# V of the eight short sequences from one stationary tile of high and low x; the memory weights cast by ScalarE; rotation buffers apart

## The reference, cut to what matters

```
proj = x @ w_in                       # 1024 -> 8192 columns
cb, cc, ch, rq, rk, rv, rg, mq, gl = split(proj)
a_out = (cb * conv3(cc * ch)) @ w_conv_out
q, k = rotary(rq), rotary(rk) * 128**-0.5;  v = rv        # 4 heads, v is 4 x 256 wide
o, new_state = retention(q, k, v, state)                  # chunks of 128, or the 8 positions
b_out = (silu(rg) * groupnorm(o)) @ w_ret_out
mk, mv = split(mem_prompt @ w_mem_kv)                     # prompt only: 256 rows x (512 + 512)
m_out = memory_attention(mq, mk, mv) @ w_mem_out
x = LN(alpha*x + (gates * (a_out, b_out, m_out)).sum() @ w_out)
x = LN(alpha*x + relu(x @ w_up)**2 @ w_down)
```

## Time and profile before

| | us |
|---|---|
| median of three runs | 2241.53 (2239.97 to 2242.13) |
| profiled execution | 2223.44 |
| its span, first to last instruction | 2221.6 |
| PE busy | 2161.7 (97%) |
| POOL busy | 1398.9 (63%) |
| DVE busy | 962.5 (43%) |
| ACT busy | 332.3 (15%) |

### The profile page before, as it was taken

The page is one execution under the profiler, slowest core; times in us unless marked ns, Lnnn a source line. Parts: engine busy times, 40 slices in busy tenths (PEclk is TensorE's granted clock), DMA queues, the critical chain, the costliest instruction groups (busy, mean ns, idle before and its releaser), DMA issues.

```text
span 2221.6 us, 39895 instructions
## 1 busy us (share of the span) xinstructions
PE 2161.7 (97%) x16468; PEld 2116.2 (95%) x16468; DVE 962.5 (43%) x1450; ACT 332.3 (15%) x584; POOL 1398.9 (63%) x1620
## 2 busy tenths in 40 slices
PE   6999999999999999999999999999999999999997
PEld 6998999999998999999999989999999989999996
DVE  6236500443368622324691562005424793324147
ACT  2122101032013100000141220010410221000002
POOL 5743558655684967767666446776456757767672
PEclk9999999999999999999999999999999999999998
DMA  4323524234321223222223153242352212222221
GB/s 159 112 76 97 169 77 134 84 105 133 115 95 58 96 76 96 76 91 80 72 63 104 58 171 114 95 125 73 106 172 78 94 58 95 77 95 76 95 76 43
DMA packets 199794, 214.96 MB, mean 97 GB/s; under 512 B 5233, under 2 KB 192625, under 8 KB 199537
## 3 DMA queue, kind: packets, MB, share of 16 engines
q1 hardware_dynamic: 168832, 170.14, 24.3%
q10 hardware_dynamic: 30832, 42.90, 5.8%
HBM read 199.06 MB, written 13.97 MB: 96 GB/s over the span
## 4 chain that ended last, share of the span: by engine, by line
PE 90%; DVE 6%; POOL 2%; issue 1%; ACT 0%; DMA 0%; POOLq 0%; ACTq 0%; SPq 0%; DVEq 0%
PE gp L405 64%; PE gp L421 7%; PE gp L431 7%; PE qb L500 6%; PE gp L556 5%; POOL w_lo L371 1%; PE qb L531 1%; DVE r L1663 1%; DVE r L1757 1%; DVE r L1666 1%; DVE x_lo L1672 1%; POOL w_hi L368 1%; PE gp L741 1%; DVE dacc L1619 0%; DVE qb L1660 0%
## 5 line engine op out<-in xcount | busy, mean ns | idle before, releaser
L371 POOL TENSOR_TENSOR w_lo<-stage,w_hi 128x256 fp32r<-128x256 f32 x1280 | 1043.0, 845 | 28.0
L368 POOL TENSOR_SCALAR w_hi<-stage 128x1024 fp32r<-128x1024 f32 (+1 forms) x336 | 358.4, 1067 | 755.1 <-PE gp L405 447.0
L405 PE MATMUL gp<-x_hi,w_hi 128*128 128x288 f32 x2176 | 465.7, 296 | 2.7 <-ACTq L955 1.7
L405 PE MATMUL gp<-x_hi,w_lo 128*128 128x288 f32 x2176 | 462.5, 294 | 0.0
L405 PE MATMUL gp<-x_lo,w_hi 128*128 128x288 f32 x2176 | 462.2, 294 | 0.0
L405 PEld LDWEIGHTS gp<-x_hi,w_hi 128*128 128x128 f32 x2176 | 348.7, 188 | 6.2 <-issue 4.5
L405 PEld LDWEIGHTS gp<-x_lo,w_hi 128*128 128x128 f32 x2176 | 348.6, 188 | 0.0
L405 PEld LDWEIGHTS gp<-x_hi,w_lo 128*128 128x128 f32 x2176 | 348.5, 188 | 0.0
L405 PE MATMUL gp<-b_hi,w_hi 128*128 128x288 f32 x1408 | 301.4, 296 | 0.0
L405 PE MATMUL gp<-b_hi,w_lo 128*128 128x288 f32 x1408 | 298.3, 293 | 0.0
L405 PE MATMUL gp<-b_lo,w_hi 128*128 128x288 f32 x1408 | 298.1, 293 | 0.0
(11 more groups left out here) (225 smaller groups left out, 3081.1 us busy)
## 6 DMA issues: line engine op xcount, KB each, us to landing
stage<-in_w_in SPq DMA_DIRECT2D x64, 1024.0 KB, 5.6
stage<-in_w_up SPq DMA_DIRECT2D x32, 1024.0 KB, 5.4
stage<-in_w_down SPq DMA_DIRECT2D x32, 1024.0 KB, 5.1
stage<-in_w_ret_out SPq DMA_DIRECT2D x8, 1024.0 KB, 5.1
stage<-in_w_mem_kv SPq DMA_DIRECT2D x8, 1024.0 KB, 5.1
stage<-in_w_out SPq DMA_DIRECT2D x8, 1024.0 KB, 5.1
s_in_c<-in_ret_state ACTq DMA_DIRECT2D x8, 512.0 KB, 4.8
out_ret_sample<-s_in_c ACTq DMA_DIRECT2D x8, 512.0 KB, 3.8
```

The lines of the kernel that those rows point to most:

```text
L368: nc.gpsimd.tensor_scalar(hi, raw, 1.0, 1.0, ALU.mult, ALU.mult).then_inc(hi_done, 1)
L371: ins = nc.gpsimd.tensor_tensor(lo[:, k:k + 2, :], raw[:, k:k + 2, :], hi[:, k:k + 2, :].bitcast(F32), ALU.subtract)
L405: last = mm(gp[:, 2 * (i % 2) + half, 0:HALF], w[:, i % 4, k * P:(k + 1) * P], x(k, half), start=(n == 0), stop=(n == 3 * nk - 1))
```

## The change

Four edits.

1. At the start of a layer ScalarE writes `x_short`: for each of the 8 row blocks the 64 short columns of `x_hi` and beside them the 64 of `x_lo`. For t = 0 TensorE takes this as the stationary operand, against `w_hi` and `w_lo`: 16 matmuls. Partitions 0 to 63 of the result hold high x times both weights, 64 to 127 low x times both. ScalarE copies the lower 64 partitions to `v_low`, and VectorE adds them to the upper ones into `v`. VectorE's four additions stand ahead of the clearing of `S` and of `qd` in its program, and TensorE waits for the last of them before the scores. The low x low product is now in the sum.
2. In T_KV ScalarE makes `w_hi` of the eight tiles (`weights_high`), GpSimd the low parts alone.
3. The two pairs of T_KV + 4 to 7 write different banks: 0 and 1, then 2 and 3.
4. `rot` moves behind `rot4`; ScalarE no longer waits for VectorE at tiles 4 and 5 of T_RQK.

```diff
-    rot = place("rot", [P, 2, 2, N], F32, a_bhi)
+    rot = place("rot", [P, 2, 2, N], F32, a_bhi + 4 * 4 * N)
     rot4 = place("rot4", [P, 4, 2, HALF], F32, a_bhi)
...
+    x_short = place("x_short", [P, KT, 2 * NS], F32R, a_r)
...
+    v_low = place("v_low", [NS, H * DV], F32, a_r + 4 * 4 * N)
@@ gpsimd
-        def split_four(l, first, rows=(KT, KT)):
+        def split_four(l, first, rows=(KT, KT), high_made=False):
...
-                if s % 2 == 0:
+                if s % 2 == 0 and not high_made:
                     pool.wait_ge(stage_full[s // 2], l * (TILES * 4) + first * 4 + 16)
...
-                nc.gpsimd.tensor_scalar(hi, raw, 1.0, 1.0, ALU.mult, ALU.mult).then_inc(hi_done, 1)
+                if not high_made:
+                    nc.gpsimd.tensor_scalar(hi, raw, 1.0, 1.0, ALU.mult, ALU.mult).then_inc(hi_done, 1)
                 pool.wait_ge(hi_done, n + s + 1)
...
-            with pool.Fori(0, T_AM // RING - 1) as it:
+            with pool.Fori(0, T_KV // RING - 1) as it:
                 split_four(l, it * RING + RING)
+            with pool.Fori(0, 2) as it:
+                split_four(l, it * RING + T_KV, high_made=True)
+            with pool.Fori(0, (T_AM - T_MQ) // RING) as it:
+                split_four(l, it * RING + T_MQ)
@@ tensor, V
+            pe.wait_ge(short_in, l + 1)
...
+                            if t == 0:
+                                for w in (w_hi, w_lo):
+                                    last = mm(out, x_short[:, k, :], w[:, i:i + 2, k * P:(k + 1) * P],
+                                              start=(n == 0), stop=(n == 2 * KT - 1))
+                                    n += 1
+                                continue
...
-                            f32(sample_out(h, g), sc[:, h, g * GT:(g + 1) * GT], v[:, 0, h * DV:(h + 1) * DV],
+                            f32(sample_out(h, g), sc[0:NS, h, g * GT:(g + 1) * GT], v[0:NS, 0, h * DV:(h + 1) * DV],
...
-            pe.wait_ge(v_ready, l * 8 + 8)
+            pe.wait_ge(v_ready, l * 4 + 4)
+            pe.wait_ge(pair_free[1], l * (TILES // 2) + T_RG // 2 + 1)
             scores(0)
@@ tensor, T_KV + 4 to 7
                 pe.wait_ge(split_done, l * TILES + t + 2 + RING)
+                pe.wait_ge(pair_free[i // 2], l * (TILES // 2) + (T_KV + 4) // 2 + 1)
                 for m in range(2):
-                    pe.wait_ge(pair_free[m], l * (TILES // 2) + t // 2 + 1)
...
-                            last = mm(gp[:, 2 * m, 0:2 * P], x[:, k, m * P:(m + 1) * P],
+                            last = mm(gp[:, i + m, 0:2 * P], x[:, k, m * P:(m + 1) * P],
@@ scalar
             act.wait_ge(x_ready[1], l * 16 + 8)
+            act_fn(x_short[:, :, 0:NS], x_hi[:, :, 0:NS].bitcast(F32), ACT.Copy)
+            act_fn(x_short[:, :, NS:2 * NS], x_lo[:, :, 0:NS].bitcast(F32), ACT.Copy).then_inc(short_in, 1)
...
-                act.wait_ge(rot_done, l * 8 + i + 1)
+                if i >= 6:
+                    act.wait_ge(rot_done, l * 8 + i + 1)
...
-                act_fn(v[:, 0, cols], gp[:, 2, 0:2 * P], ACT.Copy).then_inc(v_ready, 1)
-                act.wait_ge(v_ready, l * 8 + 2 * i + 2)
-                act.sem_inc(pair_free[1], 1)
+                act_fn(v_low[:, cols], gp[NS:P, 2, 0:2 * P], ACT.Copy).then_inc(v_low_in, 1)
...
+            def weights_high(t):
+
+                s = t % RING
+                tile_is_done(act, l, t - RING)
+                if s == 0:
+                    act.wait_ge(hi_done, l * TILES + t)
+                if s % 2 == 0:
+                    act.wait_ge(stage_full[s // 2], l * (TILES * 4) + (t - s) * 4 + 16)
+                act_fn(w_hi[:, s, :].rearrange("p (k c) -> p k c", k=KT),
+                       stage[:, s // 2, :, (s % 2) * P:(s % 2 + 1) * P], ACT.Copy).then_inc(hi_done, 1)
+
+            for i in range(4):
+                weights_high(T_KV + i)
             for i in range(4):
                 tile_is_done(act, l, T_KV + i)
                 act_fn(km[:, i, :], gp[:, 2 * (i % 2), 0:ML], ACT.Copy).then_inc(km_ready, 1)
                 act.wait_ge(km_ready, l * 8 + i + 1)
                 act.sem_inc(pair_free[i % 2], 1)
+                weights_high(T_KV + 4 + i)
             for i in (0, 2):
                 tile_is_done(act, l, T_KV + 5 + i)
                 for m in range(2):
-                    act_fn(vm[:, m, i * P:(i + 2) * P], gp[:, 2 * m, 0:2 * P], ACT.Copy).then_inc(km_ready, 1)
+                    act_fn(vm[:, m, i * P:(i + 2) * P], gp[:, i + m, 0:2 * P], ACT.Copy).then_inc(km_ready, 1)
                     act.wait_ge(km_ready, l * 8 + 4 + i + m + 1)
-                    act.sem_inc(pair_free[m], 1)
+                    act.sem_inc(pair_free[i // 2], 1)
@@ vector, ahead of the clearing of S
+            for i in range(4):
+                cols = slice(i * 2 * P, (i + 1) * 2 * P)
+                dve.wait_ge(v_low_in, l * 4 + i + 1)
+                vec_.tensor_tensor(v[0:NS, 0, cols], v_low[:, cols], gp[0:NS, 2, 0:2 * P], ALU.add).then_inc(pair_free[1], 1)
```

More of the change, by code:

```diff
@@ L262, in layers @@
     km_ready = sem("km_ready")
+    short_in = sem("short_in")
     rot_in = sem("rot_in")
@@ L265, in layers @@
     v_ready = sem("v_ready")
+    v_low_in = sem("v_low_in")
     sig_in = sem("sig_in")
@@ L968, in _ @@
                 act_fn(v[:, 1:5, cols], gp[:, 0:2, :].rearrange("p a (b c) -> p (a b) c", b=2), ACT.Copy).then_inc(v_ready, 1)
-                act.wait_ge(v_ready, l * 8 + 2 * i + 1)
+                act.wait_ge(v_ready, l * 4 + i + 1)
                 act.sem_inc(pair_free[0], 1)
                 tile_is_done(act, l, T_RV + 2 * i + 1)
-                act_fn(v[:, 0, cols], gp[:, 2, 0:2 * P], ACT.Copy).then_inc(v_ready, 1)
-                act.wait_ge(v_ready, l * 8 + 2 * i + 2)
-                act.sem_inc(pair_free[1], 1)
+                act_fn(v_low[:, cols], gp[NS:P, 2, 0:2 * P], ACT.Copy).then_inc(v_low_in, 1)
             def sigmoid(i):
```

## The result

The changed kernel took 2214.96 us (median of 4 runs, 2207.52 to 2223.05), the kernel before on the same chip 2241.68 us (4 runs, 2239.97 to 2242.13). The ratio is 0.9891 [0.9859, 0.9923]. The profiled execution took 2216.98 us (2215.2 of span), forecast 2208.4. Two errors of opposite sign, then: the profiled execution is 8.6 us slower than the sum says, the runs are 11.5 us faster.

A forecast was written before the change was run, and what follows sets the result against it. TensorE, busy 97% of the span, was taken as the bound. Terms -7.68 + 1.1 - 1.83 - 6.60 = -15.0 us took 2241.53 to 2226.5 us; the range of 8 in 10 was 2222.5 to 2231.5.

The forecast's parts named there:

- forecast 2208.4: Whole kernel, profiled execution: 2223.44 us less the 15.0 us sum of all terms.
- the last of the sum: Whole kernel: the runs' median stays 18.1 us above the profiled execution, so 2241.53 - 15.0 = 2226.5 us.
- Forecast 7.68 - 1.1 = 6.58 in all: V, both layers: 64 fewer matmuls of 0.120 us save 7.68; the hand-over before the scores costs 0.55 a layer.
- the tightest place of the forecast: Between pairs in V: the next pair's bank is free in time by 0.3 us; a 0.3 us miss would cost 1.8.
- 1.2 taken: Two ScalarE casts to x_short, start of a layer: 0.6 us each, 1.2 in all, costing TensorE 0.
- Forecast 1.83: T_RQK, layer 1: TensorE's wait for the pair goes, -1.83 us, bounds 0 to 1.83; layer 0 gains 0.
- rival (b): Layer 1's T_RQK wait becomes one for the split; at most 1.83 us lost, 2228.3 us; forecast with it 0.81.
- Forecast 3.30 a layer: Memory's keys and values: waits of 0.67 (T_KV + 4), 1.95 (T_KV + 6) and 0.68 us (T_MQ) go; 6.60 in all.
- the forecast's 0.16: TensorE's waits: each is 0.16 us longer than its row says, as a matmul is given 0.28 but costs 0.120.
- rival (a): T_KV keeps its waits, T_KV + 6 having 1.0 us of cover; 2233.1 us, or 2229.8 if half is won; chance 0.09.
- (c): T_KV: ScalarE's reads of stage slow GpSimd's subtractions; about no change, 2242 us, chance 0.04, or slower, 0.03.
- (d): V: x_short as stationary operand takes 0.180 us a matmul, losing 7.3 us; 2234.2 us; chance 0.03.

The follow-up runs named there:

- after_held: The changed kernel plus foreign matmuls of 8 and 16 columns ahead of feed-forward whole tiles 4 and 5 in both layers; 2207.44 us, ratio 0.9875.
- nudge_mm: The changed kernel plus one fp32 matmul of 64 columns between half-tile products and first whole tile of each feed-forward; 2223.71 us, ratio 0.9952.
- the held kernels: before_held and after_held, the kernel before and the changed one, each with the 8 and 16 column matmuls added; 2221.65 and 2207.44 us.
- base_again: The kernel before, unchanged, run again; 2232.56 us (median of 12), ratio 1.0002, its profiled execution 2239.5 us.
- rot_only: The kernel before with edit 4 alone (rotation buffers apart, no wait at tiles 4 and 5); one execution, 2238.33 us.
- kv_only: The kernel before with edits 2 and 3 alone (ScalarE's casts, four banks in the memory stage); 2222.93 us, ratio 0.9976.
- everywhere: two_short plus the same pair of 8 and 16 column matmuls at four more places in each layer; 2194.37 us, ratio 0.9817.
- early_scores: The changed kernel with TensorE's waits for v and the bank moved behind the first scores and half swish tile; 2205.07 us, ratio 0.9876.
- v_only: The kernel before with edit 1 alone (V's short block from 16 matmuls, with x_short and the addition); 2231.6 us, ratio 0.9993.
- two_short: early_scores plus foreign matmuls of 8 and 16 columns ahead of feed-forward whole tiles 4 and 5 in each layer; 2203.59 us, ratio 0.9857.
- before_held: The kernel before plus foreign matmuls of 8 and 16 columns ahead of feed-forward whole tiles 4 and 5 in both layers; 2221.65 us, ratio 0.9938.
- one_short: early_scores plus one foreign matmul of 16 columns ahead of feed-forward whole tile 5 in each layer; 2208.14 us, ratio 0.9871.

## Why the prediction was right and where it was wrong

**The step that failed** is the last of the sum: "The median of the runs is 18.1 us above the profiled one; I take that distance as staying". It is no constant of the program. It was the price of two feed-forwards at the long cadence (2 x 8.6 us) in the timed runs of a kernel whose profiled execution had both short; the rest of the 18.1 us is the scatter of other stages. The first four runs of the changed kernel were 2207.52 (as `after_held`, both short), 2212.94 and 2216.98 (one long; the profile of the latter shows it), and 2223.05 (as `nudge_mm`, both long). By the held kernels the 26.7 us split so: before lay 2241.68 - 2221.65 = 20.0 above its held time, after 2214.96 - 2207.44 = 7.5 above its own, together 12.5 from cadences (and a stretch at the lower clock as in `base_again`), and 14.2 from the change. The held kernels ran on a chip that may be another than that of the first result, so this split is good to a microsecond or two. The profiled execution missed its 2208.4 by 8.6 us for the same reason: layer 0's feed-forward was 8.6 us longer, and the rest of the stages that no edit touches (1.1 longer, 1.1 shorter) cancel. I had the 18.1 us in front of me and no row for it; a distance of 0.8% between a profile and three runs that agree within 0.1% wanted an explanation or a wider range.

**Edit 1.** V: 3.4 us a layer. Forecast 7.68 - 1.1 = 6.58 in all, measured 6.8: the hand-over was 0.45 us a layer, not 0.55, its addition 0.41 as the row of the nearest instruction had it. No wait arose inside V, the tightest place of the forecast. The casts took 1.25 us a layer (1.2 taken), and no wait of TensorE's came of them.

**Edit 4.** Forecast 1.83, measured 1.9 between the two profiles, 1.3 between `rot_only` and `base_again`, and 1.5 between the means of all profiles without and with it. The wait is gone from the list in each; rival (b), a wait for the split at V, is in no profile.

**Edits 2 and 3.** Forecast 3.30 a layer. `kv_only` gave 3.6 in both; the changed kernel's first profile 3.6 and 2.7. The 0.3 us more lie in the price of a wait: behind each of the three waits of the kernel before, the second distance of starts is long too (0.228, 0.224 and 0.237 us instead of 0.120 to 0.133), about 0.1 us a wait that the forecast's 0.16 left out. Layer 1 is rival (a) in small: "T_KV + 6 has 1.0 us of cover", and there it was used up. ScalarE's and GpSimd's timelines of it:

```profile
1430.35 0.39 ACT L1085 ACTIVATE km<-gp 128x256 f32<-128x256 f32 x1 [1.32 <-PE gp L746]
1432.76 1.06 ACT L1078 ACTIVATE w_hi<-stage 128x1024 fp32r<-128x1024 f32 x1 [2.03 <-DMA stage<-in_w_mem_kv]
```

```profile
1433.90 5.57 POOL L376 TENSOR_TENSOR w_lo<-stage,w_hi 128x256 fp32r<-128x256 f32 x8 [1.99 <-ACT w_hi L1078]
```

The cast stood 2.03 us for the landing, the subtraction behind it, and TensorE 0.6 us behind that. In `after_held`, `kv_only` and `everywhere` this wait is absent, in `early_scores` it is 0.7: it comes and goes with the landing.

**The rivals.** (c) is dead: subtractions of 0.70 us beside ScalarE's casts, where 4.74 / 4 = 1.19 was the price of trouble. (d) is dead: the V stage has its 448 matmuls in the time that 0.120 each gives, `x_short` as stationary tile included (447 distances in 53.6 us). What moved the time stood in none of the rivals.

**The distance of two starts.** The Trainium skill (TensorE: Matmul & The Clock Gate, Back-to-back issue gap) has columns / 2.4 + 2.5 ns for isolated matmuls, so 122.5 for 288 columns. It says itself that this doesn't hold for a stream in which each matmul has its weight load, as here, and gives for such a stream one value at 128 and one at 512 columns, neither of which is this case's shape. These traces have 130.0 and 133.3, so the measurements decide. 3.3 ns times the matmuls of one feed-forward is more than half of what this change is worth.

## What to carry to other kernels

When a profiled execution and the runs differ by more than the runs among themselves, count matmuls in a long gap-free window of each profile at hand: the same stream can have two cadences at one granted clock. Compare two versions only at equal cadence, by groups of runs or by stages, since a median over a mix has hidden 7 us (`v_only`) and added 12 (this change). Where a long gap-free stream of like tiles begins, try a pair of short matmuls of its own type, one ahead of its first tile and one ahead of its second, and read each tile's length behind them: here four of them were worth 12 us, and more of them at other stages about 10.

## What was not expected of the hardware

- A stream of 288-column matmuls, each with its weight load, runs at 130.0 or at 133.3 ns each, at granted clock 1.00, for 2616 matmuls without a change. What the two are inside the engine, and what picks one when nothing is inserted, stays open.
- Behind an fp32 matmul of 64 columns or a wait at the first whole tile the stream was long in both profiles and, by their times, in all 20 runs; behind two short matmuls of its own type (8, then 16 columns) short in the three profiles and, by their times, in all 15 runs of `two_short`, `before_held` and `after_held`. In the profiles the two do different things: the tile behind the 8 was long in all 17 places, while the 16 turned long into short in those 17 and in one of `one_short`, and short into long in the other.
- Waits of at most 2 us in T_KV were followed by a stretch of the lower clock in three of the ten such stages profiled of the kernels without edits 2 and 3 (in one the granted clock was 0.88 over 14 us; each lost 1.5 us), and in none of those with them.
